# Two attention heads in the two halves of TensorE's rows, and a 30-row first layer in four column strips

## The reference

```python
def nsa_attention(q, k_cmp, v_cmp, k_slc, v_slc, k_win, v_win, gates, ...):
    blocks = kv[:, cmp_idx] + pos_emb[:, None, :]          # 15 blocks of 32 tokens, 2 groups
    kc = jax.nn.gelu(blocks @ w1) @ w2                     # w1: 2048 x 256, w2: 256 x 64; the same for vc
    ...                                                    # softmax over the 15 compressed blocks
    # with 256 tokens "selected" and "window" are both plain causal attention, 8 heads on 2 key groups each
    out = gb[..., 0:1] * o_cmp + gb[..., 1:2] * o_slc + gb[..., 2:3] * o_win

def diff_attention(q, k, v, ...):                          # 4 heads, each the difference of two softmaxes
    a = p[:, :, 0] - lam * p[:, :, 1]
```

## Time and profile before

| | us |
|---|---|
| median of 3 runs (2435.43 to 2437.79) | 2437.32 |
| the profiled execution, its own time | 2437.86 |
| its span | 2436.1 |
| PE busy | 2160.9 (89%) |
| DVE busy | 1148.8 (47%) |
| ACT busy | 727.3 (30%) |
| L506, scores, its five shapes' busy time added | 56.9 |
| L508, mask: F matmuls, busy | 36.0 for 60 matmuls (120 instructions) |
| L1899, compression's first layer | 28.4 for 64 matmuls (128 instructions) |

### The profile page before, as it was taken

How to read it: one execution, slowest core, us unless ns; L and a number is a source line. 1 busy time by engine, 2 the same in 40 slices (tenths; PEclk the granted TensorE clock), 3 DMA queues, 4 the chain that set the end, 5 groups by cost and what they waited for, 6 DMA issues and landing times.

```text
span 2436.1 us, 30759 instructions
## 1 busy us (share of the span) xinstructions
PE 2160.9 (89%) x13048; PEld 1545.5 (63%) x13048; DVE 1148.8 (47%) x1950; ACT 727.3 (30%) x1256; POOL 71.5 (3%) x102
## 2 busy tenths in 40 slices
PE   7977999999978799999996888998997888998998
PEld 7764443333366734333343667998996767998996
DVE  4664232222166623222224565766555565766554
ACT  3731010000034200000002344543443243543442
POOL 2000000000000000000000010010000010010000
PEclk9987999999989899999997999998999999999999
DMA  8117999999951599999996412464453511454551
GB/s 297 70 66 290 428 428 427 428 427 428 418 186 70 224 390 428 427 428 428 427 427 227 173 35 78 165 216 148 160 190 121 196 47 59 163 199 157 188 188 40
DMA packets 127630, 602.47 MB, mean 247 GB/s; under 512 B 5580, under 2 KB 24144, under 8 KB 102784
## 3 DMA queue, kind: packets, MB, share of 16 engines
q1 hardware_dynamic: 122592, 589.32, 61.0%
q10 hardware_dynamic: 3920, 9.97, 1.3%
q0 software_dynamic: 976, 1.15, 0.3%
HBM read 599.37 MB, written 1.05 MB: 246 GB/s over the span
## 4 chain that ended last, share of the span: by engine, by line
PE 66%; DMA 16%; DVE 11%; ACT 5%; issue 1%; ACTq 0%; SPq 0%; DVEq 0%
PE ps L1311 12%; PE ps L414 9%; PE ps L416 9%; PE ps L415 9%; DMA rx<-in_w_up 7%; DMA ring<-in_w_up 7%; PE ps L1346 6%; ACT AB L530 2%; PE ps L427 2%; PE ps L429 2%; PE ps L428 2%; DVE ARm L908 2%; PE ps L2518 2%; PE ps L2519 2%; PE ps L2520 2%; PE ps L1249 1%
## 5 line engine op out<-in xcount | busy, mean ns | idle before, releaser
L396 DVE TENSOR_TENSOR CL<-ring,CH 128x1024 fp32r<-128x1024 f32 x284 | 332.7, 1213 | 276.4 <-ACT CH L390 276.3
L414 PE MATMUL ps<-XTH,CH 128*128 128x256 f32 x1456 | 424.9, 292 | 18.6 <-DVE CL L396 9.5
L415 PE MATMUL ps<-XTL,CH 128*128 128x256 f32 x1456 | 417.0, 286 | 0.0
L416 PE MATMUL ps<-XTH,CL 128*128 128x256 f32 x1456 | 416.7, 286 | 0.0
L390 ACT ACTIVATE CH<-ring 128x1024 fp32r<-128x1024 f32 x284 | 281.8, 1043 | 136.6 <-PE ps L2520 60.8
L414 PEld LDWEIGHTS ps<-XTH,CH 128*128 128x128 f32 x1456 | 284.9, 196 | 22.0 <-DVE XTL L458 9.9
L415 PEld LDWEIGHTS ps<-XTL,CH 128*128 128x128 f32 x1456 | 284.9, 196 | 1.1 <-issue 0.5
L416 PEld LDWEIGHTS ps<-XTH,CL 128*128 128x128 f32 x1456 | 284.6, 195 | 0.0
L1311 PE MATMUL ps<-rx,ARM 128*64 128x512 f32 x1024 | 248.7, 608 | 29.7 <-DMA rx<-in_w_up 20.4
L1311 PE MATMUL ps<-ring,ARM 128*64 128x512 f32 x1024 | 243.9, 601 | 26.1 <-DMA ring<-in_w_up 16.9
L1327 DVE TENSOR_TENSOR ARM<-ARM,ps 128x512 f32<-128x512 f32 x32 | 22.0, 687 | 455.6 <-PE ps L1311 455.6
(11 more groups left out here) (382 smaller groups left out, 3711.9 us busy)
## 6 DMA issues: line engine op xcount, KB each, us to landing
ring<-in_w_gate SPq DMA_DIRECT2D x32, 2048.0 KB, 23.9
ring<-in_w_up SPq DMA_DIRECT2D x32, 2048.0 KB, 26.9
rx<-in_w_down SPq DMA_DIRECT2D x32, 2048.0 KB, 27.1
rx<-in_w_gate SPq DMA_DIRECT2D x32, 2048.0 KB, 26.4
ring<-in_w_down SPq DMA_DIRECT2D x32, 2048.0 KB, 27.1
rx<-in_w_up SPq DMA_DIRECT2D x32, 2048.0 KB, 27.1
ring<-in_w_ffn SPq DMA_DIRECT2D x30, 2048.0 KB, 8.1
ring<-in_w_in SPq DMA_DIRECT2D x14, 2048.0 KB, 8.2
```

The costliest lines, as they stand in the source:

```text
L396: v.e.tensor_tensor(pc.lo[:, cs], pc.ap[:, cs], pc.hi[:, cs].bitcast(F), ALU.subtract).then_inc(dve_done, v.put("lo", pc.k))
L414: p.e.matmul(o, pc.hi[:, c, n0:n0 + 128], src[0][:, c, :], start=c == 0, stop=False)
L415: p.e.matmul(o, pc.hi[:, c, n0:n0 + 128], src[1][:, c, :], start=False, stop=False)
L416: m = p.e.matmul(o, pc.lo[:, c, n0:n0 + 128], src[0][:, c, :], start=False, stop=c == nk - 1)
```

## The change

1. Scores. The keys lose their zero padding (`kp` becomes `k`). Each head is a matmul of 64 rows: rows 0 to 63 for one, 64 to 127 for the other, alternating, each head into a bank of its own; both halves t of a head lie side by side in that bank.
2. Mask. It is copied once to FR (`EYE`, `MASK`, on ACT at the start), and one FR matmul per head (2 x 128 columns) adds it to both diagonal blocks.
3. Names. All scores of a job have one name, both maxima have one name, all exponentials have one name. So the first maximum waits for the job's last score, and the first exponential for the second maximum.
4. Banks. A job in slot i % 2 has banks 0 and 1 or 2 and 3 for scores; transposes always banks 4 and 5, results 6 and 7.
5. The copies and memsets that padded the keys go (DVE: one of two copies per MoBA and memory key tile, two per differential key tile; POOL: memsets).
6. Compression's first layer: the stationary operand is 32 columns wide, matmul j writes to rows 32 (j % 4) on; four partial sums are added by a matmul against `fold` (four stacked 32 x 32 identities), which also transposes. The Gelu moves behind it, to ACT, where it writes the operand of the second layer directly (`act_hidden_back`), in place of DVE's copies.

```diff
         def p_scores(j):
-            for t in range(2):
-                ks = j.keys(t)
-                o = take(("s", j.tag, t), of=j.of)[:, 0:2 * ks].rearrange("p (h k) -> p h k", h=2)
-                m = p.e.matmul(o, j.q[:, t * 128:t * 128 + 128], j.kp[:, :, 0:ks], start=True, stop=not j.causal)
-                if j.causal:
-                    m = p.e.matmul(o[:, :, 128 * t:128 * t + 128], C("ident"), bc_mid(C("cmask"), 2), start=False,
-                                   stop=True)
-                m.then_inc(pe_done, p.put("s", j.tag, t))
+
+            for h in range(2):
+                take(("s", j.tag), 2 * j.slot + h)
+            for t in range(2):
+                for h in range(2):
+                    m = p.e.matmul(score(j, t)[:, h, :], j.q[64 * h:64 * h + 64, t * 128:t * 128 + 128],
+                                   j.k[64 * h:64 * h + 64, 0:j.keys(t)], start=t == 0, stop=t == 1 and not j.causal)
+            if j.causal:
+                for h in range(2):
+                    o = banks[2 * j.slot + h].rearrange("p (t k) -> p t k", t=2)[:, :, 0:128]
+                    m = p.e.matmul(o, EYE, bc_mid(MASK, 2), start=False, stop=True)
+            m.then_inc(pe_done, p.put("s", j.tag))
...
         def v_max(j):
             for t in range(2):
-                v.wait_ge(pe_done, p.at("s", j.tag, t))
+                v.wait_ge(pe_done, p.at("s", j.tag))
                 v.own()
                 v.e.reduce_max(j.nm[:, 2 * t:2 * t + 2], score(j, t), AX.X,
-                               negate=True).then_inc(dve_done, v.put("max", j.tag, t))
+                               negate=True).then_inc(dve_done, v.put("max", j.tag))
...
-                    a.wait_ge(dve_done, v.at("max", j.tag, t))
+                    a.wait_ge(dve_done, v.at("max", j.tag))
...
         def p_turned(j):
             for t in range(2):
                 nk = j.keys(t) // 128
-                b = take(("t", j.tag, t), of=j.of)
+                b = take(("t", j.tag, t), 4 + t)
...
             for j in range(16):
-                i = p.e.matmul(b[0:30, 0:256], n.B[k][:, j].rearrange("p g n -> p (g n)"), u.ap[:, j, :], start=j == 0,
-                               stop=j == 15)
+                q = 32 * (j % 4)
+                i = p.e.matmul(b[q:q + 32, 0:256], n.B[k][:, j, :], u.ap[:, j, :], start=j < 4, stop=j > 11)
...
             for c in range(2):
-                i = p.e.transpose(b[:, c * 30:c * 30 + 30], n.HK[0:30, c * 128:c * 128 + 128], C("ident")[0:30, 0:30])
+                i = p.e.matmul(b[:, c * 32:c * 32 + 32], n.HK[:, c * 128:c * 128 + 128], C("fold"), start=True, stop=True)
...
+        def act_hidden_back(l, k):
+            n = nsas[l]
+            b = tile("hidden back", l, k)[:, 0:64].rearrange("p (c m) -> p c m", c=2)
+            a.wait_ge(pe_done, p.at("hidden back", l, k))
+            if k == 0:
+                a.e.activation(n.TK, b[:, :, 0:30], ACT.Gelu_apprx_tanh).then_inc(act_done, a.put("hidden back", l, k))
+                return
+            a.wait_ge(pool_done, g.at("zero nsa", l))
+            for c in range(2):
+                for h in range(2):
+                    a.e.activation(n.TR[:, h, c, :, 0:15], bc_mid(b[:, c, h * 15:h * 15 + 15], 4),
+                                   ACT.Gelu_apprx_tanh).then_inc(act_done, a.put("hidden back", l, k))
```

More of the change, by code:

```diff
@@ L134, with __init__ @@
 class Job:
[L137 to L139 removed]
+    def __init__(self, tag, q, k, causal, buf, gate=None, lam=None, heads=2):
+        self.tag, self.q, self.k, self.causal, self.heads = tag, q, k, causal, heads
+        self.gate, self.lam, self.before, self.value, self.slot = gate, lam, None, None, 0
         self.P, self.PT, self.sm, self.nm, self.r4 = buf
@@ L196, in program @@
         CST = sb("CST", const_np.shape[1])
+        EYE, MASK = (sb(x, 128, FR)[:, :] for x in ("EYE", "MASK"))
         SM = sb("SM", 512)
@@ L645, in g_attend, with chain @@
                     g_normed(j)
-        def chain(jobs, value, bufs, of=8):
+        def chain(jobs, value):
             for i, j in enumerate(jobs):
-                j.before, j.value, j.of = jobs[i - 2] if i > 1 else None, value[i], of
+                j.before, j.value, j.slot = jobs[i - 2] if i > 1 else None, value[i], i % 2
             return jobs
@@ L726, in act_memory @@
         def act_memory():
+            a.wait_ge(cst_in, 16)
+            a.e.activation(EYE, C("ident"), ACT.Copy).then_inc(act_done, a.put())
+            a.e.activation(MASK, C("cmask"), ACT.Copy).then_inc(act_done, a.put("mask"))
             a_transposed("mem", ms)
@@ L770, in out @@
             def out(j):
-                b = take(("out", j.tag))
+                b = take(("out", j.tag), 6 + j.slot)
                 p_values(j, b, True, True).then_inc(pe_done, p.put("out", j.tag))
@@ L1793, in program @@
                     vals.append(lambda k, h, j=j, V=V: V[:, k, (j // 2) * 64:(j // 2) * 64 + 64])
-            chain(n.jobs, vals, buf, 6)
+            chain(n.jobs, vals)
             nsas.append(n)
@@ L1844, in pe_nsa @@
             b = take(("kc", l))
+            p.wait_ge(act_done, a.at("hidden back", l, 0))
             for c in range(2):
@@ L1860, in pe_nsa @@
             b = take(("vc", l))
-            p.wait_ge(dve_done, v.at("hidden back", l, 1))
+            p.wait_ge(act_done, a.at("hidden back", l, 1))
             for h in range(2):
@@ L2114, in program @@
                 d.jobs[j].j = j
-            chain(d.jobs, [lambda k, h, j=j, V=d.V: V[:, k, j * 128:j * 128 + 128] for j in range(4)], buf)
+            chain(d.jobs, [lambda k, h, j=j, V=d.V: V[:, k, j * 128:j * 128 + 128] for j in range(4)])
             diffs.append(d)
```

97 lines of the change are left out of this document (36 added, 61 removed).

## The result

| | before | with the change |
|---|---|---|
| median, 6 runs each | 2437.56 us (2435.43 to 2439.86) | 2447.47 us (2446.10 to 2450.35) |
| ratio, 95% interval | | 1.0043 (1.003 to 1.0056) |
| profiled span | 2436.1 us | 2444.9 us |

A forecast was written before the change was run, and what follows sets the result against it. The chain was taken as mostly PE, but DVE and ACT inside NSA's loop. Convolution -0.7, MoBA +6.2, NSA -1.8 and differential +5.4 us sum to +9.1, giving 2446; range 2438 to 2457.

The forecast's parts named there:

- The joined wait: Attention loops: first exponential waits for both maxima, 0.79 us more per causal round; 5.5 per NSA layer, 2.4 differential, 5.4 MoBA.
- PE's work in the loops is worth nothing: Inside NSA's loop the chain goes round DVE and ACT; scores are ready 1.2 us early, so less PE work gains nothing.
- The first jobs: First job of each loop: +0.3 us each in MoBA and the differential loops, +2.8 per NSA layer.
- the second table load, ahead of the loop, is covered by the wait for L2066: Before NSA's loop: ACT's second table load costs nothing, hidden while the first scores wait for DVE's copy.
- The compression: NSA's compression: first layer 2.1 us instead of 7.02, twice per layer; with fold and key copy, 9.7 less per layer.
- The rule of the Trainium skill: Compression's first layer: weight loads overlap only across row groups, so 5.2 us; kernel 12 us later, 2458; chance 0.07.
- The rival with loads one after the other, 3.46: Compression's strips bound by serial weight loads, or row halves not abreast: 2452 for loads alone, 2457 together; chance 0.13.
- The convolution stage: Memory jobs' scores there halve, -1.7 us; transposes waiting for ACT's copy delay the sums of squares, +1.0.
- The ends of the loops: Loop ends in NSA and MoBA: PE's clock cold for longer, +0.5 us each.
- Rival 5: Loops really held by PE, so the joined wait is free and the kernel faster: 2434, or 2425; chance 0.09.

The follow-up runs named there:

- run 1: The kernel before, with only both maxima of a job sharing one name, so its first exponential waits for the second maximum: 2468.87 us, ratio 1.0129.
- run 2: The kernel before with the change's compression alone (four column strips, fold, Gelu behind it on ScalarE), attention untouched: 2418.72 us, ratio 0.9923.
- run 8: The changed kernel with each job's score matmuls issued twice, the second overwriting the first: 2452.03 us, ratio 1.0053.
- run 9: The changed kernel, compressed rows' transposes in bank 5, Gelus ahead of the rows' exponentials, second convolution memory job turned into bank 1: 2432.50 us, ratio 0.9977.
- run 12: The kernel of run 9 with maxima ahead of the previous job's scaling and scores one job further ahead: 2387.97 us, ratio 0.9795.
- run 4: The changed kernel with only matmul order changed: each head's two score matmuls together, each compression strip filled before the next: 2454.87 us.

## Why the prediction was right, and where it was off

The forecast was 2446, slower, for the joined wait in the loops. The time came to 2447.5, and runs 1, 2, 8 and 9 show the cause. The kind and place of every large term were right; that the sum came so near is partly luck. In the trace rounds and compression came out 5.6 lower than forecast, and the first jobs, the ends of the loops and stretches that the sum had left out 5.4 higher. Step by step:

- **The joined wait.** Right in place and kind, a little high: 0.79 was forecast, and 0.66 came (0.74 in run 1). My 1.22 for two maxima held the second one's wait for a name of its own, long fulfilled, which stands on a semaphore instruction of its own; between the two lie 0.09 in run 1 and 0.03 in the changed kernel. And the second pair of exponentials no longer waits for a name of its own either. 27 transitions gave 17.6 instead of 21.2.
- **PE's work in the loops is worth nothing.** Right (run 8).
- **The first jobs.** +0.3 was forecast and +0.4 came in the differential loop and in MoBA, but the parts were off: at the full clock the first mask starts 0.86 behind the first score, for the 0.64 forecast, and the two masks took 0.45 for 0.24 (0.22 from one to the next, not the 0.12 of the dense FR matmuls), while maxima and exponentials took a little less. In NSA two things were off. The new wait for L2066's copy came in layer 0 alone: I had carried the bank of one layer over to the other, while the turn of the banks differs. And the step "the second table load, ahead of the loop, is covered by the wait for L2066" failed: this load stands behind the semaphore instruction that waits for the maxima, and costs 1.28 in each layer. The load in MoBA's first job was covered, because there the wait for the maximum stands behind it; so the step was wrong for where the wait stands, and not because a load can't be hidden. Layer 0 lost 4.6, layer 1 2.1, where 2.8 each was forecast. The errors nearly cancel.
- **The compression.** First layers of 1.86 and 1.91 for the 2.1 forecast; four Gelus 0.56 for 1.1. 10.7 a layer, for 9.7. The rule of the Trainium skill (TensorE: Matmul & The Clock Gate, section The mechanism), by which only loads of another row group overlap, would have given 5.2 for a first layer. The trace does not agree: four strips share all rows, and 32 loads of 109 ns went by in 1.86. The rival with loads one after the other, 3.46, is out as well.
- **The convolution stage.** -1.5 for the scores, and the sums of squares start 1.2 behind ACT's L876 (1.48 from 145.88 in the chain) instead of 0.05, of -1.7 and +1.0.
- **The ends of the loops.** The term that was too small: 0.5 was forecast, 1.9 came behind MoBA and 1.4 behind NSA's layer 0. Behind a loop PE runs its last values and the next dense product at the low clock for longer. Before, MoBA's last values took 1.09 (clock 0.99 from 792 to 794), and with the change 1.98 (0.50 from 795 to 801); behind NSA's layer 0 the dense product started at 0.12 a matmul, and with the change it ran at 0.21 for 2.3 us. What keeps the clock down isn't settled. Doubling the scores warmed the loop and not MoBA's end, and behind NSA's loop the stretch to the differential loop's first score is 48.9, 50.3 or 51.6 in the traces of all runs: the kernel before has the first two of these in its two layers, and run 1, with PE's work as before, the third in both.
- **Rival 5.** One number in it is a slip: 9.1 less 21.2 from 2437.3 gives 2425, not 2434. Nothing else hangs on it.

What PE was meant to save is there: a causal job's scores and masks take 1.29 in run 12 (0.86 and 0.43), for 2.17 before. It pays only where the ring is opened; in run 12 these 1.29 stand in NSA's chain in every second round. A round of run 12 is 3.79 in the mean, and values of 0.81, transposes of 1.1 and 0.64 for the compressed part in every second round make 2.2 a job; with 2.17 for scores PE alone would need 4.4. This last is worked out from rows; whole scores with scores ahead were not run.

## What to carry to other kernels

Before joining two names, look for what ran beside what: a wait for the later one puts the whole second instruction into the ring, once per round. Work taken off an engine that isn't in the ring only makes room; to cash it in, follow the ring edge by edge, on every in-order queue (here the maxima ahead of the scaling, which alone gave little or lost, and then the scores ahead of the transposes). When functions of two tables alternate on ScalarE, reorder so that equal ones stand together. For a load that stays, look in the trace where the long wait stands: on the activation, behind the load, the load is covered by it; on a semaphore instruction ahead of the load, the load costs its full 1.28. The program's order of waits decided it here; swapping them was not run.

## What the runs showed of the hardware

- Four strips of 32 columns run fully abreast with different weights: 32 instructions of 256 columns in 1.86, for 7.02 one after the other, a factor of 3.8, though each brings its own 128-row weight load of 109 ns.
- TensorE starts matmuls for a free strip ahead of its queue's order, and up to four instructions ahead fits all distances of run 4; 16 score instructions in runs of four took 2.03 for 1.93, 32 of a first layer in runs of eight 4.52 for 1.86.
- A table load of 1.28 stands between the waits of its activation: behind those on a semaphore instruction (NSA, engine idle for 6.0 ahead of the load) and ahead of the one on the activation itself (MoBA, load over 1.27 before the exponential; L1962, 1.54).
- A second wait that has long been fulfilled costs some 0.06 on the waiting engine when it stands in the ring (0.09 for 0.03 between two maxima); it is a semaphore instruction of its own.
- Two row halves: 16 score instructions in 1.93, for 3.44 on all rows.
